# A second mixer dealt out in rounds of matmuls, and all low parts of the weights on VectorE

## The reference, cut to what matters

```python
for l in range(DEPTH):                       # DEPTH = 2
    h = h + 0.5 * rms_norm(swiglu(rms_norm(h, g1[l]), ...), g2[l])
    u = rms_norm(h, mix_pre_g[l])
    # one projection, then four branches: a short convolution (3 taps), a
    # conformer convolution (31 taps, 512 channels), differential attention
    # (4 heads), attention with forgetting (8 heads)
    merged = g0 * y_a + g1 * y_b + g2 * y_c + g3 * y_d      # g = sigmoid of projections
    h = h + rms_norm(merged @ w_o[l], mix_post_g[l])
    h = h + 0.5 * rms_norm(swiglu(rms_norm(h, g3[l]), ...), g4[l])
```

```python
def hybrid_mixer(x, ...):
    qa, ka, va, qkv_b, beta_raw, dt_raw, z, gate_raw = split(x @ w_in)
    ya = sliding_window_attention(qa, ka, va, pos_bias, sink) @ w_branch_a   # 16 heads of 64
    qkv_b = silu(causal_depthwise_conv(qkv_b, conv_w))                       # 4 taps
    qb, kb, vb = l2norm, l2norm, identity of its three parts                 # 8 heads of 128
    o = gated_delta_rule(qb, kb, vb, g, beta)    # per head, a triangular inverse in it
    o = rms(o) * dn_norm_g * silu(z);  yb = o @ w_branch_b
    return (gate_a * ya + gate_b * yb) @ w_out
```

## Time and profile before

| | |
|---|---|
| runs (us) | 3671.03, 3665.37, 3669.57; median 3669.57 |
| span of the profiled execution | 3663.0 us; 2.4 to 8.0 below the runs |
| TensorE, VectorE, ScalarE, GpSimd busy | 87%, 55%, 36%, 25% |
| weights read | 487 MB, 134 GB/s |

### The profile page before, as it was taken

One profiled execution on the slowest core, in us unless ns is written; L12 is line 12 of the kernel. 1 busy time (PEld: TensorE's weight loads), 2 busy tenths in 40 slices (PEclk: granted clock), 3 DMA queues, 4 the chain that ended last, 5 costly groups with the idle time before them and its releaser, 6 DMA issues.

```text
span 3663.0 us, 57483 instructions
## 1 busy us (share of the span) xinstructions
PE 3199.0 (87%) x22178; PEld 2990.0 (82%) x22178; DVE 2032.9 (55%) x3046; ACT 1313.3 (36%) x1898; POOL 902.9 (25%) x425
## 2 busy tenths in 40 slices
PE   7998798989998799988977778889899778778897
PEld 7988798989988798988966777789889677767897
DVE  4558766545568566554543544475555435454754
ACT  3343344333343334332333322333333333233332
POOL 0034572000054462000042333230100423332301
PEclk9998999999998899999977888899999778889899
DMA  5543344554543245556522211145455221211453
GB/s 194 185 166 104 105 152 163 185 176 157 184 165 101 96 146 174 184 170 203 197 93 70 70 58 63 62 158 188 167 184 196 92 71 69 70 58 64 160 185 126
DMA packets 72104, 495.34 MB, mean 135 GB/s; under 512 B 8000, under 2 KB 8176, under 8 KB 19856
## 3 DMA queue, kind: packets, MB, share of 16 engines
q1 hardware_dynamic: 67504, 471.95, 37.8%
q0 software_dynamic: 4048, 18.59, 2.0%
q10 hardware_dynamic: 272, 0.99, 0.1%
HBM read 487.31 MB, written 4.19 MB: 134 GB/s over the span
## 4 chain that ended last, share of the span: by engine, by line
issue 67%; POOL 17%; PE 7%; DVE 4%; DVEq 1%; ACT 1%; POOLq 1%; DMA 1%; ACTq 0%; SPq 0%
POOL weights_low L851 15%; PE psum L947 6%; POOL small L811 1%; DMA weight_ring<-stream 1%; PE psum L950 1%; DVEq L2145 1%; DVE small L1938 1%; DVE normed_t_low L1759 1%; ACT weights_high L1433 0%; DVE normed_t_high L1757 0%; POOLq L810 0%; POOL work L899 0%; POOLq L873 0%; POOL residual L874 0%; DVE work L2051 0%
## 5 line engine op out<-in xcount | busy, mean ns | idle before, releaser
L947 PE MATMUL psum<-normed_t_high,weights_high 128*128 128x256 f32 x4832 | 1410.1, 292 | 36.3 <-DVE normed_t_low L1759 32.5
L947 PE MATMUL psum<-normed_t_low,weights_high 128*128 128x256 f32 x4832 | 1390.9, 288 | 0.0
L947 PE MATMUL psum<-normed_t_high,weights_low 128*128 128x256 f32 x4832 | 1389.1, 287 | 0.0
L1433 ACT ACTIVATE weights_high<-weight_ring 128x2048 fp32r<-128x2048 f32 (+1 forms) x464 | 859.3, 1856 | 1461.6 <-DMA weight_ring<-stream 1453.9
L1750 DVE TENSOR_TENSOR weights_low<-weight_ring,weights_high 128x2048 fp32r<-128x2048 f32 x292 | 672.3, 2306 | 697.3 <-ACT weights_high L1433 694.8
L947 PEld LDWEIGHTS psum<-normed_t_high,weights_high 128*128 128x128 f32 x4832 | 953.2, 197 | 49.7 <-DVE normed_t_low L1759 37.0
L947 PEld LDWEIGHTS psum<-normed_t_low,weights_high 128*128 128x128 f32 x4832 | 953.1, 197 | 4.5
L947 PEld LDWEIGHTS psum<-normed_t_high,weights_low 128*128 128x128 f32 x4832 | 951.0, 197 | 0.0
L851 POOL TENSOR_TENSOR weights_low<-weight_ring,weights_high 128x2048 fp32r<-128x2048 f32 (+1 forms) x172 | 725.1, 4219 | 875.0 <-ACT weights_high L1433 875.0
L947 PE MATMUL psum<-weights_high,work_parts 128*128 128x512 f32 x1664 | 524.3, 396 | 13.2 <-DVE work_parts L1759 13.2
L947 PE MATMUL psum<-work 128*128 128x128 f32 (+3 forms) x2000 | 358.6, 330 | 113.7 <-DVE work L2199 45.4
(11 more groups left out here) (187 smaller groups left out, 2489.0 us busy)
## 6 DMA issues: line engine op xcount, KB each, us to landing
weight_ring<-stream SPq DMA_DIRECT2D x400, 1024.0 KB, 4.8
weight_ring<-stream SPq DMA_DIRECT2D x64, 768.0 KB, 4.2
feature_rows<-feat POOLq DMA_DIRECT2D x6, 1024.0 KB, 4.9
work<-toeplitz_rows POOLq DMA_DIRECT2D x8, 512.0 KB, 7.1
feature_rows<-feat POOLq DMA_DIRECT2D x6, 512.0 KB, 4.0
toeplitz_rows<-work POOLq DMA_DIRECT2D x1, 3072.0 KB, 36.0
params<-prms POOLq DMA_DIRECT2D x5, 251.5 KB, 3.1
residual<-x SPq DMA_DIRECT2D x1, 1024.0 KB, 7.5
```

The source lines that it names most:

```text
L947: return pe.matmul(dst, lhsT, rhs, start=start, stop=stop, skip_group_check=True)
L1433: return act.activation(dst, src, ACT.Copy, scale=scale)
```

## The change

Three things change. All low parts of weights are made by VectorE (`by_pool` is empty). The second mixer's dense units in the attention and delta stages are no longer placed whole: `interleave` deals their 16 rounds out evenly behind the chain steps, as steps of kind `part`; the last part of a unit is the unit's own step. The order of units in these stages is another: query and convolution units in the first half of the attention, the `pz` units in the second, in a head pair the convolutions first and the two gates behind. And a split may now be asked for in quarters of a unit. `mm`, `transpose` and `cols_product` are written out where they stood, with the same matmuls.

```diff
+QUARTERS = 4
@@ class Plan
-        self.by_pool = ("w", "ba", "aa", "gy")
+        self.by_pool = ()
@@ close
-        used, split, short = 0, 0, True
+        used, high, low, short = 0, 0, 0, True
         for n, st in enumerate(self.steps):
-            used += st.unit is not None
-            if st.unit is not None:
-                short = any(x.kind in ("post", "post2") for x in self.steps[n + 1:n + 3])
-            upto = min(used + AHEAD - short, self.units) if used or st.kind in ("norm", "xt") else 0
-            while split < upto:
-                st.split.append(split)
-                split += 1
+            if st.kind == "part":
+                used += st.a == 0
+                at = QUARTERS * (used + 1) + QUARTERS * st.a // st.src.rounds
+                to_high, to_low = at + 1, at
+            else:
+                if st.unit is not None:
+                    used += st.first == 0
+                    short = any(x.kind in ("post", "post2") for x in self.steps[n + 1:n + 3])
+                ahead = 1 if st.first else AHEAD - short
+                to_high = QUARTERS * (used + ahead) if used or st.kind in ("norm", "xt") else 0
+                to_low = to_high
+            last = QUARTERS * self.units
+            if min(to_high, last) > high:
+                st.high, high = quarters(high, min(to_high, last)), min(to_high, last)
+            if min(to_low, last) > low:
+                st.low, low = quarters(low, min(to_low, last)), min(to_low, last)
@@ new
+def interleave(pl, chain, dense):
+    total = sum(rounds for rounds, _ in dense)
+    given, done, later = 0, 0, []
+    todo, host = list(dense), None
+    for n, f in enumerate(chain):
+        f()
+        if later:
+            later.pop(0)()
+        upto = total * (n + 1) // len(chain)
+        while given < upto:
+            if host is None:
+                rounds, make = todo.pop(0)
+                host, rest = make()
+                done = 0
+            give = min(upto - given, host.rounds - done)
+            if done + give < host.rounds:
+                pl.steps.append(Step("part", None, src=host, a=done, b=done + give))
+            else:
+                host.first = done
+                pl.steps.append(host)
+                later += rest
...
@@ plan_second
-    dense = [project_q[2:4] + project_z[0:2], project_z[2:4] + [lambda w=w: conv(0, w) for w in range(3)]]
+    dense = [[(16, lambda p=p: query(p)) for p in (2, 3)] + [(16, lambda w=w: conv(0, w)) for w in range(3)],
+             [(16, lambda p=p: gated(p)) for p in range(4)]]
...
-        weave(pl, chain, evenly(chain, dense[half]))
+        interleave(pl, chain, dense[half])
...
-        convs = [lambda w=w, hp=hp: conv(hp + 1, w) for w in range(3)] if hp + 1 < NH_B // 2 else []
-        dense = {1: gates[2 * hp:2 * hp + 1], 3: gates[2 * hp + 1:2 * hp + 2]}
-        dense.update({pos: [g] for pos, g in zip((15, 23, 31), convs)})
-        weave(pl, chain, dense)
+        dense = [(16, lambda w=w, hp=hp: conv(hp + 1, w)) for w in range(3)] if hp + 1 < NH_B // 2 else []
+        dense += [(16, lambda k=k: gate(0, k)) for k in range(2 * hp, 2 * hp + 2)]
+        interleave(pl, chain, dense)
@@ split_high on ScalarE; split_low in the same way
-                copy(HIGH[:, i % SLOTS, 0:width(i)], RING[:, i % SLOTS, 0:width(i)]).then_inc(high_ready, 1)
+                copy(some(HIGH, i, q, n), some(RING, i, q, n)).then_inc(high_ready, n)
```

More of the change, by code:

```diff
@@ new lines, in close, with quarters @@
+            last = QUARTERS * self.units
[3 more added lines that the diff above has]
+                st.low, low = quarters(low, min(to_low, last)), min(to_low, last)
+        assert high == low == QUARTERS * self.units
+def quarters(a, b):
+    out = []
+    while a < b:
+        n = min(b, (a // QUARTERS + 1) * QUARTERS)
+        out.append((a // QUARTERS, a % QUARTERS, n - a))
+        a = n
+    return out
@@ L200, in weave @@
             later += rest if isinstance(rest, list) else []
+    for g in later:
+        g()
+def interleave(pl, chain, dense):
[19 more added lines that the diff above has]
+                later += rest
+            given, done = given + give, done + give
+            if done == host.rounds:
+                host = None
+    assert host is None and not todo
     for g in later:
@@ L381, in plan_second @@
             signals=[("small_proj_ready", 1), ("small_logs_ready", 1), ("log_decay_ready", 1)])
-    project_q = [lambda p=p: pl.step("pq", ("pq", p), banks=["lo"], p=p, unit=("w", p)) for p in range(4)]
-    project_q[0]()
-    project_q[1]()
+    for p in range(2):
+        pl.steps.append(query(p)[0])
     pl.step("pv", "pv", banks=["lo"], unit=("w", 5))
@@ L420, in plan_second, with gate @@
                 signals=[("activation_high_ready", 2)])
[L422 to L425, removed]
-            gates.append(lambda i=i, k=k, last=last: pl.step(
-                "gy", ("gy", i, k), banks=["lo"], i=i, k=k, unit=("gy", i, k),
-                signals=[("gate_tanh_ready", 1)] + last))
+    def gate(i, k):
+        last = [("merged_ready", 1)] if i == 1 else []
+        return pl.make("gy", ("gy", i, k), banks=["lo"], i=i, k=k, unit=("gy", i, k),
+                       signals=[("gate_tanh_ready", 1)] + last), []
     for hp in range(NH_B // 2):
@@ L1050, in pb @@
[L1050 to L1070 removed]
+                w = weights(st, KB, a == 0)
@@ new lines, in product @@
+                if a == 0:
+                    pe.wait_ge(bank_taken[job.bank], turn_at(job))
+                for r in range(a, b):
+                    c, k = r // KB, r % KB
+                    if fresh is not None and c == 0 and k % 2 == 0:
+                        ready = named(("xt", fresh)).jobs[k // 2]
+                        pe.wait_ge(bank_taken[ready.bank], taken_at(ready))
+                    for m, (i, j) in enumerate(PARTS):
+                        ins = pe.matmul(PS[:, job.bank, c * S:(c + 1) * S], w[i][:, k, c * P:(c + 1) * P], XT[j][:, k, :],
+                                        start=(k, m) == (0, 0), stop=(k, m) == (KB - 1, 2), skip_group_check=True)
+                        if (r, m) == (0, 0):
+                            pay(ins)
@@ new lines, in project, with project_tokens, part @@
+            def project(st, fresh=None):
+                product(st, st.first, st.rounds, fresh)
+            def project_tokens(st):
+                product_by_tokens(st, st.first, st.rounds)
+            def part(st):
+                host = st.src
+                if host.kind == "gy":
+                    gate_product(host, st.a, st.b)
+                elif host.kind in ("pv",) or host.what in ("cv", "dv"):
+                    product_by_tokens(host, st.a, st.b)
+                else:
+                    product(host, st.a, st.b)
@@ L1244, in wo @@
+                if b == st.rounds:
+                    ins.then_inc(bank_full[job.bank], 1)
+                    owed[0] += 1
             def wo(st):
@@ L1334, in dl0 @@
                 for t in range(T):
-                    ins = mm(PS[:, job.bank, t * P:(t + 1) * P], MT[:, i, t, :], IDENT)
+                    ins = pe.matmul(PS[:, job.bank, t * P:(t + 1) * P], MT[:, i, t, :], IDENT, start=True, stop=True, skip_group_check=True)
                     if t == 1:
```

286 lines of the change are left out of this document (149 added, 137 removed).

## The result

The changed kernel takes 3753.99 us (median of 4 runs, 3751.66 to 3756.01); the kernel before, in the same comparison, 3669.11 us. The ratio is 1.0229 (95% interval 1.0215 to 1.0244): slower by 85 us where 28 was forecast. The profiled execution's span is 3754.3 us against 3663.0.

A forecast was written before the change was run, and what follows sets the result against it. It took VectorE to bound the first mixer and a chain of short TensorE, ScalarE or VectorE steps the second. Per layer -18 - 6 + 40 - 2 = +14, +28 for both: 3663.0 + 28 + 6.6 = 3698 us, range 3600 to 3800.

The forecast's parts named there:

- the quarters that never occur: Second mixer: chain steps ask for whole units up to three ahead, so every conversion and subtraction stays 128x2048 or 128x1536.
- the walk: Step-by-step timing of units with trace durations: 95.7 us for a head pair, 78 and 56 for the attention halves.
- First mixer, -18 a layer: First mixer: subtractions move to VectorE and held taps are freed, 140 us instead of 160; bounds -29 and 0.
- Price of the place: Second mixer: behind a unit's first matmul, ScalarE is shut until +7.3 us and VectorE until about +9.7; the chain waits.
- its mark: Second mixer: ScalarE's wait for the ring's loads grows, about 7 us behind each unit's first matmul.
- Delta stage, +40: Delta stage, per layer: three head pairs of 101 us and a last of 63, 366 against 326.2; bounds -10 to +79.
- 2.4 for matmuls behind the waits that run at the lower clock: Delta stage: allowance of 2.4 us a head pair for slower matmuls, bringing 98.6 to 101.
- Attention, -6: Second mixer's attention, per layer: 134 us against 144, less 4 for the clock; bounds -25 and +15.
- less 4 for the clock in the gaps: Attention stage: 4 us of the 10 us gain taken off for lower clock in gaps, leaving -6.
- Rival B, the clock: Delta and attention stages: freezes leave TensorE's clock low, under 0.7 over delta; +16 us a pair, total 3804; chance 0.17.
- the main case: Whole kernel: freezes slow the delta stage, partly offset by first mixer and attention; 3698 us, own range 3665 to 3735.
- Rival C, full dealing, 3380: Second mixer: dealing works fully wherever splits stand; a pair at 60 us, attention at 100, total 3380; chance 0.06.

The follow-up runs named there:

- e1: The kernel before, with VectorE making the low parts in the first block only: 3615.42 us, ratio 0.9849.
- e4: The changed kernel, but chain steps among dealt rounds ask for no splits, only the parts do, in quarters: 3429.58 us, ratio 0.9342.
- e6: e4, with the second block's low parts made by GpSimd, in quarters too: 3420.58 us, ratio 0.9319.
- e10: The changed kernel, but dealt chain steps ask for low parts two units ahead, conversions still three ahead: 3613.33 us, ratio 0.9853.
- e1b: e1, with VectorE also making the second block's low parts except the gates'; whole units in the old order: 3608.29 us, ratio 0.9831.
- e7: The changed kernel, new order of units kept, but each unit stands whole at the place of its first rounds: 3664.19 us, ratio 0.9992.
- e5: The changed kernel, but the whole split three units ahead hangs on a unit's last part and no other dealt step asks: 3464.12 us, ratio 0.9439.
- e3: The changed kernel, but chain steps among dealt rounds ask for whole splits two units ahead instead of three: 3508.28 us, ratio 0.9564.
- e9: e6, with splits in the first mixer asked for two units ahead instead of three: 3401.08 us, ratio 0.9266.
- e2: The changed kernel, with GpSimd making the low parts as before and the dealing kept: 3686.91 us, ratio 1.005.

## Why the prediction was wrong

The direction, the quarters that never occur, and the mechanism were right; the size was a third of what came. Two terms of the sum failed. The delta stage's lacked most of what TensorE's lower clock costs: 7.7 us a pair, where 2.4 were allowed. The attention's lacked it too, and besides it set the walk against a stretch 7 us too long.

- *First mixer, -18 a layer.* Right in kind, and too small: 24.2 and 25.8, inside the bounds. This error hid 14 us of the others. The taps fell to 0.466 us as said, and e1 shows that nothing else takes part.
- *Price of the place.* Right: ScalarE free at +7.3 and VectorE at +9.7 behind a unit's first matmul were forecast; in the unit shown they are free 6.7 and 9.1 us behind the load's issue, which comes some 0.5 us later than that matmul. What I named as its mark, a longer wait of ScalarE for the ring, did not come (75 and 79 us): the wait did not grow, it moved in front of the chain. VectorE's wait for the conversion, the other mark, did come: 96.0 us in 15 waits.
- *Delta stage, +40.* Mis-sized: +57 in the first layer, about +64 in the second, its last pair and the end included. All five units of a pair came out 1.3 to 2.3 us longer than the walk: from subtraction to subtraction, in order, 20.9, 22.7, 23.0, 20.5 and 18.3, where it had 18.6, 21.4, 21.1, 18.2 and 16.4. The sum is 9.7 more than the walk's 95.7, of which the forecast allowed 5.3 (3% and the clock's 2.4). A miss as even as that does not look like a forgotten wait. The term that failed is "2.4 for matmuls behind the waits that run at the lower clock". For the second pair, the changed kernel and e4:

```profile
2108.83:2214.74 105.91, 67.89 (x461) 64.85 (x459) 48.10 (x124) 27.42 (x70) 6.54 (x12) 0.79 0.15 50
```

```profile
2037.42:2107.35 69.93, 60.15 (x461) 57.01 (x459) 48.09 (x138) 28.18 (x84) 7.07 (x12) 0.95 0.22 76
```

  The same 461 matmuls take 67.9 us instead of 60.2: 7.7 us of lower clock, where 2.4 were allowed. The difference, 5.3, is what lies between the 101 of the forecast and the 106 measured. The idle time agrees: 105.9 less 67.9 is 38.0 us, and the forecast's 101 less 60.2 and 2.4, an estimate with e4's busy time for the walk's, is 38.4. The walk had durations at the full clock; the 88 us it was set against held the slow ones of a kernel at 0.87.
- *Attention, -6.* The other term that failed, with the wrong sign: +10.2 and +11.0, inside its bounds, 16 to 17 us off the forecast. First, the walk's 134 us, with 1 for the start, were set against the 144 of the earlier trace rows. That stretch begins at 1897, the first exponential comes at 1904.4, and from there the kernel before takes 137.1: 7 us of the miss lie in this comparison. Second, counted from the first exponential the forecast is 134 + 4 = 138, and the two halves, 78 and 56 in the walk, took

```profile
1855.28:1937.62 82.34, 56.44 (x337) 50.70 (x336) 34.41 (x86) 26.73 (x64) 0.00 (x0) 0.76 0.15 52
1937.62:2002.61 64.99, 51.42 (x304) 46.58 (x304) 20.61 (x56) 23.62 (x58) 0.00 (x0) 0.79 0.19 65
```

  I put these 9 us down to the same step as in the delta stage: "less 4 for the clock in the gaps". The changed kernel's 638 matmuls of this stage are busy 107.5 us (the second row of stretches above), those of e6

```profile
1854.78:1958.20 103.42, 90.97 (x638) 82.93 (x639) 36.59 (x132) 51.32 (x142) 41.77 (x24) 0.89 0.24 82
```

  91.0: 16.5 for the 4 allowed, enough for the 9 us and more if all of it lay on the path. Apart from the forecast, the runs show what VectorE's wait for the conversion is worth here: 147 dealt with it, 122 to 126 dealt without it (e10); with it beside whole units 131 (e1b) or 124 (e7). That the lower clock's share lies on the path, in this stage and in the delta stage, was worked out from busy times and not run by itself.
- *Rival B, the clock.* Its sign, a clock under 0.7 over the delta stage, did not come: it was 0.78, and TensorE was busy no longer than before. Its price was 16 us a pair; 7.7 came. So the truth lies between the main case and B, and 3754 lies between their 3698 and 3804. e4 deals the same rounds at 0.96, so it is the gaps and not the dealing that lower the clock.
- *Rival C, full dealing, 3380.* It was given 0.06 on the ground that no order hides the load's 5.4 us from a ScalarE that waits for it. For this kernel it did not happen, but the ground was wrong: asked a few steps later (e5) or a unit nearer (e3, e4), ScalarE does not wait for it. e9 comes within 21 us of that number.

The sum, with what was measured: for a layer -25 (first mixer), +10.6 (attention), +60 (delta stage with its last pair), about 0 in the rest: +46, and 91 for both, which is the difference of the profiled spans; the medians of the runs differ by 85.

## What to carry to other kernels

Work dealt out in small pieces needs its preparations placed anew: look, in the order of the changed kernel, at which short step now stands behind a wait that used to lie beside a long one. Ask for a buffer's split when its load has landed, not when the load may start; here that alone turned 85 us of loss into 160 us (e3) or 206 us (e5) of gain, with whole splits; quarters gave more (e4, 239 us). When a plan says quarters, count the instructions by size: the rule that asked for more from another kind of step had swallowed them.

## What the runs showed of the hardware

TensorE's busy time for the same matmuls of three head pairs was 205 us with gaps (clock 0.78) and 178 us nearly without (0.96). Of the 113 us that e4 gains there over the changed kernel, 27 are the clock's and 86 idle time: closing gaps pays about a third on top of the gap itself.

VectorE's 2.29 us subtraction cost nothing a unit beside a whole dense unit (e1b against e1, pairs of 88 to 92 against 85 to 94). In front of an answer of the chain it cost little as long as its conversion was done: with all five of a pair there, e10 takes 89 to 92 us, and 95 with them on GpSimd and asked three units ahead (e2). What cost 16 us a pair was the wait of 5.4 to 6.8 us in front of each.
